# Expert layer of a transformer block: 32 tokens' up products by gather, their tile's gate weights added in memory

## The reference

```
q = (ht @ peer_wq).reshape(T, 8, 2, 128)
s = einsum('thpd,hpkd->thpk', q, peer_keys)        # scores against 128 keys, twice
sv, si = top_k(s, 16)
cand, cidx = all 16 x 16 sums of the two halves, and i * 128 + j
top, pos = top_k(cand, 16);  eidx = cidx at pos
g = softmax(top)
a = gelu(einsum('td,thkd->thk', h, peer_u[eidx]))  # 8 heads x 16 picks a token
out = einsum('thk,thkd->td', g * a, peer_v[eidx])
```

## Time and profile before

| | us |
|---|---|
| median of 3 runs | 1614.82 |
| lowest, highest | 1613.53, 1616.74 |
| the profiled execution | 1616.59 |
| its span | 1614.8 |
| TensorE, VectorE busy | 1589.7, 1338.9 |
| ScalarE, GpSimd busy | 635.4, 407.1 |

### The profile page before, as it was taken

The page is one execution under the profiler, slowest core; times in us unless marked ns, Lnnn a source line. Parts: engine busy times, 40 slices in busy tenths (PEclk is TensorE's granted clock), DMA queues, the critical chain, the costliest instruction groups (busy, mean ns, idle before and its releaser), DMA issues.

```text
span 1614.8 us, 24652 instructions
## 1 busy us (share of the span) xinstructions
PE 1589.7 (98%) x8490; PEld 1386.0 (86%) x8490; DVE 1338.9 (83%) x2533; ACT 635.4 (39%) x978; POOL 407.1 (25%) x343
## 2 busy tenths in 40 slices
PE   8998999999999999999999999999999999999998
PEld 5776677887889999999998888888888888888887
DVE  6899787665699999999678888888888888888876
ACT  4432834235334445544433333333333333333332
POOL 0000101101434300000244433343334333443320
PEclk9999999999999999999999999999999999999999
DMA  8431155652424567877999998999989999999981
GB/s 324 155 105 33 46 197 195 222 184 103 157 79 134 159 202 245 261 267 226 377 414 402 350 337 330 347 347 354 343 335 328 360 361 339 335 322 363 356 307 71
DMA packets 168012, 418.79 MB, mean 259 GB/s; under 512 B 12673, under 2 KB 78337, under 8 KB 167810
## 3 DMA queue, kind: packets, MB, share of 16 engines
...
## 4 chain that ended last, share of the span: by engine, by line
PE 90%; DVE 5%; ACT 2%; DMA 1%; issue 1%; DVEq 0%; ACTq 0%
PE bank L1575 16%; PE bank L1577 16%; PE bank L1576 16%; PE bank L1921 11%; PE bank L1922 11%; PE bank L1920 11%; PE bank L1899 3%; DVE sb_scr L1086 2%; DMA sb_scr<-w_ada_dram 1%; PE bank L1831 1%; DVE sb_w_lo L973 1%; DVE sb_scr L987 1%; PE bank L1738 1%; PE bank L1607 1%; PE bank L1609 1%
## 5 line engine op out<-in xcount | busy, mean ns | idle before, releaser
L625 ACT ACTIVATE sb_w_hi<-sb_stage 128x1024 fp32r<-128x1024 f32 x324 | 343.3, 1061 | 540.6 <-PE bank L1922 322.3
L973 DVE TENSOR_TENSOR sb_w_lo<-sb_stage,sb_w_hi 128x1024 fp32r<-128x1024 f32 x294 | 359.4, 1224 | 173.4 <-ACT sb_w_hi L625 162.1
L1575 PE MATMUL bank<-sb_act_hi,sb_w_hi 128*128 128x384 f32 (+1 forms) x1408 | 498.1, 354 | 2.9 <-DVE sb_w_lo L973 2.2
L1577 PE MATMUL bank<-sb_act_hi,sb_w_lo 128*128 128x384 f32 (+1 forms) x1408 | 492.7, 350 | 0.0
L1576 PE MATMUL bank<-sb_act_lo,sb_w_hi 128*128 128x384 f32 (+1 forms) x1408 | 492.3, 350 | 0.0
L1922 PE MATMUL bank<-sb_w_hi,sb_mix_lo 128*128 128x512 f32 x768 | 300.1, 391 | 0.0
L1921 PE MATMUL bank<-sb_w_lo,sb_mix_hi 128*128 128x512 f32 x768 | 299.9, 390 | 0.0
L1920 PE MATMUL bank<-sb_w_hi,sb_mix_hi 128*128 128x512 f32 x768 | 298.9, 389 | 0.0
L1575 PEld LDWEIGHTS bank<-sb_act_hi,sb_w_hi 128*128 128x128 f32 x1408 | 264.4, 188 | 23.4 <-issue 4.4
L1576 PEld LDWEIGHTS bank<-sb_act_lo,sb_w_hi 128*128 128x128 f32 x1408 | 264.5, 188 | 17.2 <-issue 0.5
L1577 PEld LDWEIGHTS bank<-sb_act_hi,sb_w_lo 128*128 128x128 f32 x1408 | 264.2, 188 | 15.2
...
## 6 DMA issues: line engine op xcount, KB each, us to landing
sb_stage<-u_dram SPq DMA_DIRECT2D x128, 512.0 KB
sb_stage<-v_dram SPq DMA_DIRECT2D x128, 512.0 KB
...
```

The lines of the kernel that those rows point to most:

```text
L625: nc.scalar.activation(w_hi[:, slot, :], stage[:, slot, :], ACT.Copy).then_inc(w_round, 1)
L973: nc.vector.tensor_tensor(w_lo[:, slot, :], stage[:, slot, :], w_hi[:, slot, :].bitcast(F32), ALU.subtract).then_inc(w_split, 1)
L1575: nc.tensor.matmul(out, w_hi[:, slot, w], rhs_hi[:, dc, :], start=(i == 0), stop=False)
L1577: last = nc.tensor.matmul(out, w_lo[:, slot, w], rhs_hi[:, dc, :], start=False, stop=(i == len(dcs) - 1))
```

## The change

The last 32 of the third tile's tokens (NS = 32; ST = 2 is the tile) leave the dense up products: a slab's matmuls have NU = 352 columns instead of 384. Their 32 x 128 picks are gathered in 32 indirect DMAs of 128 rows (four groups of 32 tokens on the partitions; SPICKS = 32), with 32 dots by VectorE (sparse_dot) and one gelu. The down products stay dense for them, with 1.0 in the place of the activation (ga[:, :, NU:ND]).

The whole third tile leaves the gate turns: G_TURNS is 2, with 16 slabs each, a batch a slab, from slab 24 on. Its part of g_scratch is zeroed (four DMAs by GpSimd, 8 MB), and its weights are added to it in memory: 128 indirect DMAs with compute_op add for 96 tokens (dense_add: a DMA for each pick, one element a token), 32 of 128 elements for the 32 (sparse_add: weight times gelu). Between heads GpSimd waits for the adds before to have landed. g_scratch is laid out by partition first.

The third tile's top-k and indices come first (ORDER), so the last tile's stand behind a wait for GpSimd's splits, with splits in between. GpSimd's split is four instructions of 256 columns. Fewer taps stand among the head norms, and six gate units instead of five go before the merge (GATES_FIRST).

```diff
-GATES_FIRST = 5
+GATES_FIRST = 6
...
-Y_SUM, Y_SQ, Y_OUT = MIX0 + 5, MIX0 + 6, MIX0 + 2 * GATES_FIRST
+Y_SUM, Y_SQ, Y_OUT = MIX0 + 6, MIX0 + 7, MIX0 + 2 * GATES_FIRST
...
+NS = 32
+NU = ND - NS
+GROUPS = P // NS
+SPICKS = PICKS // GROUPS
+ST = DT - 1
+ORDER = (ST, 0, 1, GT)
+LISTS_BEFORE = {ST: 0, 0: 0, 1: 1, GT: 2}
+S_ROWS = 6
...
-EXP_SLAB = 15
+EXP_SLAB = 20
+EXP_FIRST = 8
 POOL_SLABS = 16
-LIST_SLAB = 18
-LIST_UNIT = 9
-PIECE_UNITS = (0, 1, 3, 4, 6, 7, 8)
-G_FIRST = 20
-G_UNITS = 12
+POOL_PARTS = 4
+LIST_SLAB = 22
+LIST_UNIT = 13
+PIECE_UNITS = ((1, 3, 5, 7, 9, 11, 12), (6, 8, 9, 10, 11, 13, 14))
+G_FIRST = 24
+G_UNITS = 16
...
-G_TURNS = ND // TURN_TOKENS
+G_TURNS = DT - 1
+DOT_UNITS = 22
+WEIGHT_UNIT = 26
...
-                            sp.wait_ge(gw_out[i], 16 * ND // TB // 2)
+                            sp.wait_ge(gw_out[i], 16 * G_TURNS * TURN_TOKENS // TB // 2)
+                        sp.wait_ge(d_out, 16 * PICKS)
+                        sp.wait_ge(s_out, 16 * SPICKS)
...
+            nc.gpsimd.memset(zeros, 0.0).then_inc(gz_ok, 1)
+            pool.wait_ge(gz_ok, 1)
+            for k in range(4):
+                pool.dma_start(g_d[:, 8 * k:8 * k + 8, 4 * ST:4 * DT, :].rearrange("p a n m -> p a (n m)"),
+                               zeros.rearrange("p (o m) -> p o m", o=1).to_broadcast([P, 8, 4 * P])).then_inc(gz_in, 16)
...
                     pool.nop(nofuse=True)
-                nc.gpsimd.tensor_tensor(w_lo[:, slot, :], stage[:, slot, :], w_hi[:, slot, :].bitcast(F32),
-                                        ALU.subtract).then_inc(w_split, 1)
+                for k in range(POOL_PARTS):
+                    part = slice(k * D // POOL_PARTS, (k + 1) * D // POOL_PARTS)
+                    last = nc.gpsimd.tensor_tensor(w_lo[:, slot, part], stage[:, slot, part], w_hi[:, slot, part].bitcast(F32),
+                                                   ALU.subtract)
+                last.then_inc(w_split, 1)
...
+            nc.gpsimd.memset(ga[:, :, NU:ND], 1.0).then_inc(one_ok, 1)
...
+            g_flat = g_d.rearrange("p a n m -> (p a n m)").rearrange("(r o) -> r o", o=1)
+
+            def dense_add(h, r):
+                k = r * PH + h
+                pool.indirect_dma_start(g_flat, bass.IndirectOffsetOnAxis(ap=m_list.bitcast(U32)[0:P - NS, 1, k:k + 1], axis=0),
+                                        m_list[0:P - NS, 2, k:k + 1], None, compute_op=ALU.add).then_inc(d_out, 16)
+
+            def sparse_add(h, r):
+                k = r * PH + h
+                pool.indirect_dma_start(g_flat, bass.IndirectOffsetOnAxis(ap=s_list.bitcast(U32)[:, 1, k:k + 1], axis=0),
+                                        s_w[:, k:k + 1], None, compute_op=ALU.add).then_inc(s_out, 16)
+
+            def sparse_gather(k):
+                if k >= S_ROWS:
+                    pool.wait_ge(s_used, k - S_ROWS + 1)
+                pool.indirect_dma_start(s_row[k % S_ROWS], None, u_rows_d,
+                                        bass.IndirectOffsetOnAxis(ap=s_list.bitcast(U32)[:, 0, k:k + 1], axis=0)
+                                        ).then_inc(sg_in[k % S_ROWS], 16)
+
+            pool.wait_ge(st_ok, 1)
+            for g in range(GROUPS):
+                pool.dma_start(s_list[g * NS:(g + 1) * NS, :, :],
+                               m_list[P - NS:P, :, g * SPICKS:(g + 1) * SPICKS]).then_inc(sl_in, 16)
+            pool.wait_ge(gz_in, 64)
+            for h in range(PH):
+                if h:
+                    if h == 1:
+                        pool.wait_ge(sl_in, 16 * GROUPS)
+                    for k in range((h - 1) * 5, min(h * 5, SPICKS)):
+                        sparse_gather(k)
+                    pool.wait_ge(d_out, 16 * TOPK * h)
+                for r in range(TOPK):
+                    dense_add(h, r)
+            assert (PH - 1) * 5 >= SPICKS
+            pool.wait_ge(sw_ok, 1)
+            for h in range(PH):
+                if h:
+                    pool.wait_ge(s_out, 16 * SPICKS // PH * h)
+                for r in range(SPICKS // PH):
+                    sparse_add(h, r)
...
                 act.wait_ge(ks_ok, c + 1)
+                if c == 0:
+                    act.wait_ge(gz_in, 64)
...
-                    nc.scalar.activation(ga[:, k % 2, :], UB[k][:, 0:ND], ACT.Gelu).then_inc(ge_ok, 1)
+                    nc.scalar.activation(ga[:, k % 2, 0:NU], UB[k][:, 0:NU], ACT.Gelu).then_inc(ge_ok, 1)
...
-                for tt in range(TT if q == EXP_SLAB else 0):
-                    act.wait_ge(tk_ok, tt + 1)
+                for tt in ORDER[:1] if q == EXP_FIRST else ORDER[1:] if q == EXP_SLAB else ():
+                    act.wait_ge(tk_ok, ORDER.index(tt) + 1)
...
-                    if b == LIST_UNIT + 1 and it + 1 < DT:
+                    if it * G_UNITS + b == WEIGHT_UNIT - 1:
+                        act.wait_ge(s_used, SPICKS)
+                        nc.scalar.activation(s_gelu, s_dot, ACT.Gelu).then_inc(sd_ok, 1)
+                    if b == LIST_UNIT + 1 and it + 1 < G_TURNS:
...
-                        done = conv(done, (4, 3, 2, 3, 3, 2, 3, 2)[m])
+                        done = conv(done, (2, 2, 2, 2, 2, 2, 2, 1)[m])
...
-                done = conv(done, 6)
+                done = conv(done, 4)
...
-                    if tt == GT:
+                    if tt in (ST, GT):
...
+                    if tt == ST:
+                        link(nc.vector.tensor_copy(ranku[:, 0, :], j3))
...
+                        mark(nc.vector.scalar_tensor_tensor(out=m_list.bitcast(U32)[:, 1, :], in0=i3, scalar=float(NKEY * ND),
+                                                            in1=rstart, op0=ALU.mult, op1=ALU.add))
+                        link(nc.vector.tensor_copy(m_list[:, 2, :], ijw[tt % 2][:, 2, :]))
+                        nc.vector.memset(small[:, 60:61], 0.0).then_inc(st_ok, 1)
...
+            for half in range(2):
+                dve.wait_ge(ht2_ok, DC // 2 * (half + 1))
+                nc.vector.tensor_copy(s_h[:, half * 512:half * 512 + 512], UB[2 + half][:, :]).then_inc(hs_cp, 1)
             for h in range(PH):
-                topk_pair([(0, h), (1, h)])
+                topk_pair([(ST, h), (0, h)])
                 if h % 2:
-                    topk_pair([(2, h - 1), (2, h)])
+                    topk_pair([(1, h - 1), (1, h)])
+            below_top(ST)
+            dve.wait_ge(ro_ok, 1)
+            dve.wait_ge(x2_out, 16)
+            for piece in range(7):
+                indices(ST, piece)
+            dve.wait_ge(w_split, POOL_LAST)
             for h in range(0, PH, 2):
                 topk_pair([(GT, h), (GT, h + 1)])
-            for tt in range(TT):
+                for n in (POOL_LAST + h, POOL_LAST + h + 1):
+                    split_unit(n, n % RING)
+            for tt in ORDER[1:]:
                 below_top(tt)
-            dve.wait_ge(ro_ok, 1)
-            dve.wait_ge(w_split, POOL_LAST)
-            dve.wait_ge(x2_out, 16)
             link(nc.vector.tensor_copy(ident16, ident))
             for piece in range(7):
-                if piece % 2 == 0:
-                    split_unit(POOL_LAST + piece // 2, (POOL_LAST + piece // 2) % RING)
+                if piece in (2, 5):
+                    n = POOL_LAST + PH + (piece == 5)
+                    split_unit(n, n % RING)
                 indices(0, piece)
...
+            dve.wait_ge(hs_cp, 2)
 
             def early_dot(g):
                 dot(EARLY_ROWS[g % 3], g // 3 + 1, dot_early[:, g:g + 1])
+
+            def sparse_dot(k):
+                dve.wait_ge(sg_in[k % S_ROWS], 16 * (k // S_ROWS + 1))
+                nc.vector.tensor_tensor_reduce(s_row[k % S_ROWS], s_row[k % S_ROWS], s_h, 1.0, 0.0, ALU.mult, ALU.add,
+                                               s_dot[:, k:k + 1]).then_inc(s_used, 1)
+
+            def sparse_weights():
+                dve.wait_ge(sd_ok, 1)
+                dve.wait_ge(sl_in, 16 * GROUPS)
+                nc.vector.tensor_tensor(s_w, s_list[:, 2, :], s_gelu, ALU.mult).then_inc(sw_ok, 1)
...
-                    if b in PIECE_UNITS:
-                        indices(it + 1, PIECE_UNITS.index(b))
-
-            for n in (4, 5):
-                split_unit(POOL_LAST + n, (POOL_LAST + n) % RING)
+                    u_ = it * G_UNITS + b
+                    for k in range(min(u_ * SPICKS // DOT_UNITS, SPICKS), min((u_ + 1) * SPICKS // DOT_UNITS, SPICKS)):
+                        sparse_dot(k)
+                    if u_ == WEIGHT_UNIT:
+                        sparse_weights()
+                    if b in PIECE_UNITS[it]:
+                        indices((1, GT)[it], PIECE_UNITS[it].index(b))
...
+                    for g in range(GROUPS):
+                        last = nc.tensor.matmul(UB[2 + m // 4][g * NS:(g + 1) * NS, m % 4 * P:(m % 4 + 1) * P],
+                                                wide[:, m, NU:ND], ident, start=True, stop=True)
+                    last.then_inc(ht2_ok, 1)
...
+                if c == 2:
```

(41 more changed lines are left out.)

39 lines of the change are left out of this document (25 added, 14 removed).

## The result

The changed kernel takes 1742.16 us (median of 4 runs, 1740.37 to 1749.21; the profiled execution 1740.81) beside 1615.78 of the kernel before; the ratio of the times is 1.079, 95% interval 1.077 to 1.081. The forecast was 1655, range 1594 to 1700. The direction was right, the size was not: 126 us slower instead of some 40.

A forecast was written before the change was run, and what follows sets the result against it. TensorE and VectorE were both full in the gate stage, TensorE in the laps; GpSimd's serial chain was the new limit. 1616.6 + 64 (late slab 64) - 20.5 (laps) - 5 (attention front) = 1655 us, 80% range 1594 to 1700.

The forecast's parts named there:

- its four terms: Gate stage, VectorE's work: units 113.9, sparse dots 39.0, indices 11.7 and 14.5; together 179.7 us, ending at 783.4.
- the price of GpSimd's chain: Gate stage: 1.5 us per GpSimd add or gather, issued serially; VectorE stands 36 us and leaves the stage at 821.
- the sparse part: After the dense adds: three heads at 8.0 us, five at 7.0, ending at 853; TensorE stands 25 us.
- 64 - 5 = 59: Ahead of the laps: slab 64 at 877.7 instead of 813.7, +64 us; fewer taps in the attention front, -5 us.
- The tail: Between gate stage and laps: eight slabs up to slab 64, at 4.16 us each before and 3.84 after.
- rival B: GpSimd's adds are cheap (0.83 us) and never late; slab 64 at 814, total 1592, up to 1605; chance 0.27.
- C: GpSimd's adds are slow to land or issue (pitch 2.25, landing 5.1); slab 64 near 940, 1700 or more; chance 0.13.
- rival A: GpSimd's delay beside VectorE is chance, every issue costs 1.24 us; slab 64 at 854, +40, total 1631; chance 0.14.

## Why the prediction was wrong

**Right:** a slab got 0.32 us shorter and the laps 21.0 (20.5 forecast). The taps gave 6.3 us at slab 0 (488.47 instead of 494.75; forecast 5). Quarters cost nothing. TensorE stood some 16 us in four places up to 595, 11.2 of it for the lists and the rest ahead of slabs whose splits VectorE had late (forecast 18 in one piece for the lists, from 583 to 601). VectorE's own work in the gate stage was sized to within a few us: without adds the last gate product starts at 782.7. The forecast was 783.4; its four terms add to 179.1 and not 179.7, which gives 782.8, and with the 5 us of the taps taken off it is 778. The mechanism of the loss was named in its order: late rows of u, TensorE idle ahead of slab 59, the releaser VectorE's split, behind it the early row, behind that the adds.

**The step that failed** is the price of GpSimd's chain: "I take 1.5, with 1.24 and 2.25 as ends". The value came from gathers in the laps, beside a VectorE that is 84% busy. In the gate stage VectorE is fuller, and its instructions there are large two-operand ones: without adds the 32 gathers there take 1.50 on average, 1.80 with the gap. And an add is not a gather: 1.41 alone against 0.94, and 2.09 beside VectorE. Its mean with the gap is 2.02, so 128 of them take 258.7 instead of 192, 67 us more. The dense adds ended at 846 instead of 792, VectorE waited 92 us for rows instead of 38, and the gates ended at 871 instead of 821 (787 and 816 with the taps taken off). The rows that the value rested on the earlier trace rows hold gathers only. The writes without addition show which part of the price is the addition's: 0.50 of 1.41 where VectorE stands.

**A second term of the same step** is the sparse part, "a head is four issues and then a wait for landing: ... I take 2". It took 82 us (846 to 928) instead of the 58 (795 to 853) forecast. A head's four issues took 7.1 where VectorE stood (6.0 at the forecast's price), and up to 9.8 beside it. The wait for landing was 1.7 to 1.8 us at a DMA share of 0.27 or less, near the 2 forecast, but 5.6 and 5.9 in two places at 1.18 and 0.83. At the laps' first product 86 us are missing (145.2 measured, 64 - 5 = 59 forecast). Both terms together put slab 59 at 935.1 instead of 858.5, or 853.5 with the taps taken off: 81.6 of them. The other 4.6 lie between slab 59 and the laps, 28.1 us instead of 23.5: behind the long wait TensorE's granted clock is 0.50 until 940, which costs some 2.4, and it waits 2.5 ahead of the first product of the laps.

**The tail** was treated as eight slabs that TensorE runs without standing. There are nine, as one up product of the laps comes ahead of their first down product; that cancels in a difference. What does not cancel is that shorter slabs meet transfers that were hidden before: the tail took 37.8 us before, 38.3 with shorter slabs alone and 45.8 without adds. This is why rival B's 1592 would not have come either: with adds that cost nothing at all, the measured kernel is at 1604.5. That is 16 us above the kernel before with 32 tokens' up products merely left out (1588.7), although it has the gain of the taps as well: the dots, gathers and reordering take back more than the dropped gate turn gives.

**The rival that came nearest** is C, adds slow to issue and to land, for 1700 or more, at a chance of 0.13. Its price, a pitch of 2.25 and a landing of 5.1, was nearly the price of adds beside VectorE (2.39, and up to 9.2 from issue to landing). I had said what spoke for it, that no row of the trace showed a read and a write of 4 bytes in memory, and still took the middle of the gathers.

**Who hinders whom.** The forecast weighed a rule of the Trainium skill, "SBUF — State Buffer", "Who interferes with whom", by which a two-input VectorE instruction would not hold GpSimd's descriptor generation, against one row of the trace. The runs decide against that inference for these indirect DMAs: adds of one form take 1.41 to 1.47 us while VectorE stands (37 of them) and 1.95 on average beside its large two-operand instructions (62). Whether it is the writing of descriptors that is held, or another step of an issue such as reading the indices, was not tested. By rival A's price of 1.24 for each, the chain of 192 would have been 238 us; measured are 385.
